# State-space stage of a decoder block: a rotated real scan on VectorE in place of eight levels of shifted matmuls

## What is computed

```python
# 32 groups of 16 channels, 64 complex states for each group, 2048 positions
a_bar = jnp.exp(lam * dt)                          # (32, 64) complex
b_bar = ((a_bar - 1.0) / lam)[..., None] * b
bu = jnp.einsum('bsgc,gpc->bsgp', uf.astype(jnp.complex64), b_bar)
_, states = lax.associative_scan(combine, (a_seq, bu), axis=1)   # s[t] = a_bar * s[t-1] + bu[t]
y = jnp.einsum('bsgp,gcp->bsgc', states, c).real + d_skip * uf
```

## Time and profile before

| what | us |
|---|---|
| median of 3 runs | 3365.31 (3364.07 to 3366.06) |
| the profiled execution | 3363.57 |
| its span in the trace | 3361.8 |
| busy in the span: PE, PEld | 3075.7, 2599.8 |
| busy in the span: DVE, ACT, POOL | 1742.0, 1119.1, 589.3 |

### The profile page before, as it was taken

One profiled execution on the slowest core, in us unless ns is written; L12 is line 12 of the kernel. 1 busy time (PEld: TensorE's weight loads), 2 busy tenths in 40 slices (PEclk: granted clock), 3 DMA queues, 4 the chain that ended last, 5 costly groups with the idle time before them and its releaser, 6 DMA issues. The chain is left out here.

```text
span 3361.8 us, 43581 instructions
## 1 busy us (share of the span) xinstructions
PE 3075.7 (91%) x16178; PEld 2599.8 (77%) x16178; DVE 1742.0 (52%) x2451; ACT 1119.1 (33%) x1919; POOL 589.3 (18%) x387
## 2 busy tenths in 40 slices
PE   6999918969999987995999699999999899999998
PEld 5888816759889976774788578888888788888887
DVE  5333357557778764545566444444444544444444
ACT  4333214537677663312343221111111211111111
POOL 1212246825555541210000000000000000000000
PEclk9999958979999998997999899999999999999999
DMA  4233261072322205414122431111111411111111
GB/s 162 82 89 86 68 84 27 26 179 70 79 54 48 57 15 124 119 63 179 53 94 82 144 112 45 50 50 50 50 50 50 151 50 50 50 50 50 50 37 63
DMA packets 230223, 251.42 MB, mean 75 GB/s; under 512 B 107456, under 2 KB 181184, under 8 KB 230080
## 3 DMA queue, kind: packets, MB, share of 16 engines
q1 hardware_dynamic: 230096, 249.74, 25.3%
HBM read 189.79 MB, written 58.73 MB: 74 GB/s over the span
## 5 line engine op out<-in xcount | busy, mean ns | idle before, releaser
L2474 DVE TENSOR_TENSOR f_y<-f_ps_down,f_y 128x1024 f32<-128x1024 f32 x256 | 313.3, 1224 | 324.4 <-PE f_ps_down L2584 324.4
L2417 ACT ACTIVATE f_act_f<-f_ps_up 128x512 f32<-128x512 f32 x128 | 76.5, 598 | 1030.1 <-PE f_ps_up L2568 1030.1
L2566 PE MATMUL f_ps_up<-f_ht_hi,f_up_hi 128*128 128x512 f32 x1024 | 400.8, 391 | 6.4 <-DVE f_act_f L2491 6.4
L2582 PE MATMUL f_ps_down<-f_down_hi,f_a_hi 128*128 128x512 f32 x1024 | 400.6, 391 | 6.1 <-issue 6.1
L2567 PE MATMUL f_ps_up<-f_ht_lo,f_up_hi 128*128 128x512 f32 x1024 | 400.1, 391 | 0.0
L2568 PE MATMUL f_ps_up<-f_ht_hi,f_up_lo 128*128 128x512 f32 x1024 | 400.0, 391 | 0.0
L2583 PE MATMUL f_ps_down<-f_down_lo,f_a_hi 128*128 128x512 f32 x1024 | 399.9, 390 | 0.0
L2584 PE MATMUL f_ps_down<-f_down_hi,f_a_lo 128*128 128x512 f32 x1024 | 399.7, 390 | 0.0
L690 POOL TENSOR_TENSOR a_w<-a_on,a_left 128x640 f32<-128x640 f32 (+5 forms) x192 | 282.1, 1469 | 254.8 <-DVE a_left L740 113.3
L2491 DVE SCALAR_TENSOR_TENSOR f_act_f<-f_ps_up,f_act_f 128x512 f32<-128x512 f32 x128 | 88.5, 691 | 393.4 <-ACT f_act_f L2417 393.4
L828 PE MATMUL a_ps_y<-a_wt,a_v 128*96 128x128 f32 x2176 | 271.3, 274 | 3.7 <-DVE a_yt L763 3.7
(11 more groups left out here) (319 smaller groups left out, 5738.4 us busy)
## 6 DMA issues: line engine op xcount, KB each, us to landing
f_up_raw<-in_w_up SPq DMA_DIRECT2D x32, 1024.0 KB, 5.3
f_down_raw<-in_w_down SPq DMA_DIRECT2D x32, 1024.0 KB
p_xt<-in_x SPq DMA_DIRECT2D x16, 512.0 KB, 4.8
q<-p_qt SPq DMA_DIRECT2D x16, 512.0 KB, 3.2
k<-p_qt SPq DMA_DIRECT2D x16, 512.0 KB, 3.2
a_q<-q SPq DMA_DIRECT2D x16, 512.0 KB, 5.5
a_k_hi<-k SPq DMA_DIRECT2D x32, 256.0 KB, 8.2
a_k_lo<-k SPq DMA_DIRECT2D x32, 256.0 KB, 9.1
```

The costliest lines, as they stand in the source:

```text
L2474: dve.tensor_tensor(y[:, t, :], down_ps[t % 2][:, :], y[:, t, :], ALU.add).then_inc(added.sem, 1)
L2566: pe.matmul(o, up_hi[:, k, cols], ht_hi[:, k, rows], start=(k == 0), stop=False)
L2582: pe.matmul(o, a_hi[par][:, s, rows], down_hi[:, s, cols], start=(s == 0), stop=False)
```

## The change

In place of the level matrices, the scan is made of real numbers. A chunk's factor is written as `rho` times a rotation. Turning the state of chunk n back by n rotations leaves a recurrence with the real factor `rho`, the same at each step, which `tensor_tensor_scan` on DVE does along the free axis; the result is turned forward again. For this the kernel needs a table of the cosine and the sine of n rotations, for each state and each of 256 chunks.

- Setup: `dbl` is gone. `t_in` and `mat_out` are each made by three or four DVE operations of 4096 elements, `mat_out` all on DVE. DVE makes the first 64 entries of the table for all groups (`low`, by doubling) and the rotations by 64 and 128. ACT copies `mat_in`, a second matrix `mat_in_j` (states with real and imaginary part exchanged) and `kern`. PE makes the exchanged `mat_out_j` in 8 further matmuls through the single bank `o_ps`, ACT copying each out.
- For each pair: ACT copies 64 entries into `table` and multiplies by the rotation (`parts`, four operations for each of two levels), POOL adds the products up to 128 and then to 256 entries (`grow`, two operations for each level). PE makes v and its exchanged form (`make_v`, 4 matmuls in place of 2). DVE multiplies both by the table and adds (`tilt`, `add`), and scans (2 scans of 256). POOL multiplies the result by cosine and by sine (`rotate`, 2 operations of 510 elements). PE makes y with 6 matmuls in place of 4. The 32 matmuls of the levels are gone.
- `u` is kept in three buffers of 8 groups, in place of all 32 groups.

The core of the diff:

```diff
-                pool.tensor_tensor(turned_part[:, :, :], swap[:, None, :].to_broadcast([P, LEVELS, P]),
-                                   dbl[:, :, 1, g:g + 1].to_broadcast([P, LEVELS, P]), ALU.mult
...
-                pool.tensor_tensor(a_mat[g // 2 % 4][:, g % 2, :, :], plain_part[g % 2][:, :, :], turned_part[:, :, :],
-                                   ALU.add).then_inc(a_ready, 1)
...
+            def grow(p):
+                t = table[p % TS]
+                pool.wait_ge(low_copied, p + 1)
...
+                for level, m in enumerate((LO, 2 * LO)):
+                    pool.wait_ge(part_ready, 8 * p + 4 * level + 4)
+                    by_s, by_c = part[:, :, 0, :, 0:m], part[:, :, 1, :, 0:m]
+                    pool.tensor_tensor(t[:, 0, :, m:2 * m], by_c[:, 0, :, :], by_s[:, 1, :, :], ALU.subtract).then_inc(grown, 1)
+                    pool.tensor_tensor(t[:, 1, :, m:2 * m], by_c[:, 1, :, :], by_s[:, 0, :, :], ALU.add).then_inc(grown, 1)
+            def rotate(p):
+                pool.wait_ge(scanned, 2 * p + 2)
...
+                pool.tensor_tensor(s_cos[p % RS][:, :, 1:CHUNKS], t[:, 0, :, 0:CHUNKS - 1], now, ALU.mult
+                                   ).then_inc(rotated, 1)
+                pool.tensor_tensor(s_sin[p % RS][:, :, 1:CHUNKS], t[:, 1, :, 0:CHUNKS - 1], now, ALU.mult
+                                   ).then_inc(rotated, 1)
+            grow(0)
+            grow(1)
+            for p in range(PAIRS):
+                rotate(p)
+                if p + 2 < PAIRS:
+                    grow(p + 2)
...
+            def parts(p):
...
+                act.activation(t[:, :, :, 0:LO], low[:, :, 2 * p:2 * p + 2, :], ACT.Copy).then_inc(low_copied, 1)
+                for level, (m, turn) in enumerate(((LO, turn64), (2 * LO, turn128))):
+                    if 2 * p + level:
+                        act.wait_ge(grown, 4 * p + 2 * level)
+                    for i in range(2):
+                        g = 2 * p + i
+                        src = t[:, :, i, 0:m] if level else low[:, :, g, :]
+                        for by, x in ((0, 1), (1, 0)):
+                            act.activation(part[:, :, by, i, 0:m], src, ACT.Copy, scale=turn[:, x, g:g + 1]
+                                           ).then_inc(part_ready, 1)
...
+            for p in range(PAIRS):
+                if p + 2 < PAIRS:
+                    parts(p + 2)
+                copy_y(p)
...
+            def tilt(p):
+                dve.wait_ge(v_made, p + 1)
+                dve.wait_ge(grown, 4 * p + 4)
...
+            for p in range(PAIRS + 1):
+                if p < PAIRS:
+                    tilt(p)
+                if p >= 1:
+                    scan(p - 1)
+                if p < PAIRS:
+                    add(p)
...
+            for n in range(G // 4):
+                if n >= 1:
+                    pe.wait_ge(crossed_copied, n)
+                mm = pe.matmul(o_ps[:, :].rearrange("p (g l c) -> p g l c", g=4, c=C), swap[:, :], mat_out[:, 4 * n:4 * n + 4, 1:SUB + 1, :],
+                               start=True, stop=True)
+                mm.then_inc(crossed_made, 1)
...
+            for p in range(PAIRS):
+                if p == 0:
+                    make_v(2)
+                    pe.wait_ge(within_in, SUB * DMA)
+                elif p + 2 < PAIRS:
+                    make_v(p + 2)
+                make_y(p)
```

More of the change, by code:

```diff
@@ L884, in ssm_scan @@
-        kern = sb("kern", [C, G, P])
+        mat_out_j = sb("mat_out_j", [P, G, SUB * C])
+        t_in = mat_out_j[:, :, :].rearrange("p g (l c) -> p g l c", c=C)
         mat_within = sb("mat_within", [P, G, P])
[L886 to L897, removed]
+        u = sb("u", [P, US, 8, CHUNKS])
+        table = [sb(f"table{i}", [P, 2, 2, CHUNKS]) for i in range(TS)]
@@ L974, in _ @@
[L974 to L986, removed]
@@ L1006, in _ @@
             act.activation(num[:, 7, :], num[:, 5, :], ACT.Sin, scale=0.5).then_inc(sines, 1)
[L1007 to L1017, removed]
@@ L1048, in stt, with both @@
                 link(dve.scalar_tensor_tensor(out, a, x, b, op0, op1))
-            ROUND = 12582912.0
+            def both(*instructions):
+                for ins in instructions[:-1]:
+                    ins.then_inc(dve_link, 1)
+                    link.n += 1
+                link(instructions[-1])
             def exp_of(out, x, k, r):
@@ new lines, in _ @@
+            dve.wait_ge(in_rows, 1)
+            both(dve.tensor_copy(turn8[:, 0, :], num[:, 9, :]), dve.tensor_copy(turn8[:, 1, :], num[:, 6, :]))
+            for _ in range(3):
+                squared(turn8, turn8)
+            normalise(one(turn8), 1, None)
+            link(dve.tensor_copy(low[:, :, :, 0], turn8[:, :, :]))
+            m = 1
+            while m < LO:
+                first, last = low[:, :, :, 0:m], low[:, :, :, m - 1:m]
+                straight, crossed = [wide[:, i * 2 * G * m:(i + 1) * 2 * G * m].rearrange("p (a g n) -> p a g n", a=2, g=G)
+                                     for i in range(2)]
+                both(dve.tensor_tensor(straight, first, last[:, 0:1, :, :].to_broadcast([P, 2, G, m]), ALU.mult),
+                     dve.tensor_tensor(crossed, first, last[:, 1:2, :, :].to_broadcast([P, 2, G, m]), ALU.mult))
+                both(dve.tensor_tensor(low[:, 0, :, m:2 * m], straight[:, 0, :, :], crossed[:, 1, :, :], ALU.subtract),
+                     dve.tensor_tensor(low[:, 1, :, m:2 * m], straight[:, 1, :, :], crossed[:, 0, :, :], ALU.add))
+                m *= 2
+                if m == 16:
+                    normalise(low[:, :, :, 0:m], m, None)
@@ new lines, in _ @@
+            link(dve.tensor_copy(turn64[:, :, :], low[:, :, :, LO - 1]))
+            normalise(one(turn64), 1, None)
+            squared(turn128, turn64)
+            normalise(one(turn128), 1, None)
+            dve.engine_nop().then_inc(low_ready, 1)
+            dve.wait_ge(in_turned, G // 4)
+            c_of = [cc[:, x, :].rearrange("p (g c) -> p g c", c=C) for x in range(2)]
+            above = pw[:, 1:SUB + 1, :, :]
+            both(dve.tensor_copy(mat_out[:, :, 0, :], c_of[0]),
+                 dve.tensor_tensor(mat_out[:, :, 1:, :], by_row(c_of[0]), by_power(above, 0), ALU.mult),
+                 dve.tensor_tensor(wide4, by_row(c_of[1]), by_power(above, 1), ALU.mult))
@@ new lines, in add, with scan @@
+            def add(p):
+                dve.wait_ge(tilted_j, p + 1)
+                dve.wait_ge(tilted_v, p + 1)
+                dve.tensor_tensor(two(v_ps[p % VS]), two(v_ps[p % VS]), tilted[p % 2][:, :, :], ALU.add).then_inc(added, 1)
+            def scan(p):
+                dve.wait_ge(added, p + 1)
+                if p >= SS:
+                    dve.wait_ge(rotated, 2 * (p - SS + 1))
+                for i in range(2):
+                    g = 2 * p + i
+                    dve.tensor_tensor_scan(sigma[p % SS][:, i, :], rho[:, g:g + 1].to_broadcast([P, CHUNKS]),
+                                           v_ps[p % VS][:, i * CHUNKS:(i + 1) * CHUNKS], 0.0, ALU.mult, ALU.add
+                                           ).then_inc(scanned, 1)
```

324 lines of the change are left out of this document (175 added, 149 removed).

## The result

The changed kernel takes 3374.7 us (median of 7 runs, 3372.8 to 3381.3), the kernel before took 3365.4 beside it (7 runs, 3363.9 to 3371.2). The ratio is 1.0025, with a 95% interval of 1.0015 to 1.0035: slower by 9 us, a little more than the 0.2% that I took as the least that can be told. The profiled execution took 3373.3 us, its span is 3371.5.

What follows compares the result with a forecast made beforehand. PE bounds the loop before, a closed chain across engines afterwards. Loop start 565.2, plus 8.7 to scan 1, 118.0 for 13 periods and 13.5 at the end: 705.4 us, 14.9 later, so 3380.2 us; range 3364 to 3394.

Steps and rivals of the forecast that it cites:

- Setup: Steps ahead of the exchange: `in_rows` at 489.5 us, table's end 516.6, `mat_out` 531.4, `kern` copied by 541.4.
- rival of dear wide operations: Setup: the six stepped 4096-element operations of `t_in` and `mat_out` cost 0.5 ns an element more, +12 us: 3392; chance 0.13.
- Exchange: Before the loop: eight matmuls and copies through one bank cannot overlap; at PE's lower clock they take 19.3 us.
- X: Time when the loop proper starts, behind the exchange: 565.2 us, or 559.2 at 2.4 GHz.
- The chain: Pair loop: rotation, `grow` with ACT's products, tilt and scans run in series, 9.08 us a pair; 13 periods take 118.0 us.
- Tail: Behind scan 14: rotation 14, two `make_y` of 12 instructions each at the lower clock, and the copy, 13.5 us.
- lower bound of 8.0 us: The end of the stage behind scan 14, with PE at 2.4 GHz: 8.0 us in place of 13.5.
- the open chain: Rival in the loop: the chain does not close, POOL's 4.5 us a pair sets the pace, saving 60 us: 3320; chance 0.10.
- PE as the bound: Rival in the loop: PE at the lower clock takes 9.8 us a pair, +9 us more, 3389; chance 0.08.

Runs made afterwards that it cites:

- two-bank run: The changed kernel with the eight exchange matmuls of mat_out going through two PSUM banks in turn, in place of one: 3365.9 us, ratio to before 0.9997.
- scan-first run: The changed kernel with DVE's queue having the scan of a pair ahead of the tilt of the next one: 3342.5 us, ratio to before 0.9928.

## Why the prediction was right

Forecast 3380, measured 3375, and slower as said. The last copy of y was due to end at 705.4 us and ends at 702.9, so 12.4 us later than before where 14.9 were due. In the profiled executions the forecast is 5.2 us too high: 2.5 of it are in the stage, 2.4 in the later stages, which I had taken as equal. Part of how close the number comes is luck, since errors in it offset each other. Point by point:

- **Setup:** `in_rows` due at 489.5, PE's first transpose starts at 490.7; table's end due at 516.6, found at 517.5; `mat_out` due at 531.4, found at 531.5; `kern` copied at 541.4, found at 540.9. Here two errors offset: `t_in` ends 1.1 us late (`bb` starts at 473.3, not 472.1), `mat_out` and `kern` together take 1.4 less than due. The rival of dear wide operations is refuted by 4.42 us where 4.45 was due.
- **Exchange:** due 2.68 us apart at the lower clock, found 2.76. X due at 565.2, found 564.9. The step from there to the first scan's end was 8.2 us, 8.7 due. The two-bank run shows the term by itself.
- **The chain:** 9.08 us a pair due, 9.16 found, link by link in the period shown above. Two errors offset each other. The rotation, priced by L690, was 0.26 us too cheap; L273's shortest, 1.27 us in the same group, was the right row, which I kept as a bound. The 1.3 us that I set beside it and gave to the Trainium skill do not follow from its figure alone: 2.6 cycles an element at the 1.2 GHz with which the same section works are an estimated 1.1 us (GPSIMD Engine Reference, 3.1 Elementwise — side-by-side cycle accounting). The trace agrees with that figure as a slope: L273 and L1483 are 1124 ns apart for 512 elements, an estimated 2.6 cycles each, and leave 0.15 us for each operation. Slope and fixed part together are an estimated 1.27 us for 510 elements, near the 1.26 found. L690 is another line, 638 ns at 256 and 1091 at 512, an estimated 2.1 cycles an element. The other links with their crossings were together 0.18 us too dear. Thirteen periods took 119.4 us, 118.0 were due; one of the thirteen is 9.51 us long, since its tilt starts 0.44 us behind POOL's L1005 and not 0.09; what it waited for is open.
- **Tail:** the term that was mis-sized, 13.5 us due, 10.4 found. I had put all 24 matmuls at the lower clock. The trace has a granted clock of 0.50 from 695 to 698 us and 1.00 from 699 to 702: PE, busy without pause, gets the clock back in the middle of the burst. My lower bound of 8.0 us was added up wrongly, its own terms make 8.4; this bound and my value bracket what was found.
- **Rivals:** the open chain did not happen in the change, and the scan-first run shows what it is worth, 32 us rather than the 60 that I gave it. My 60 took POOL's busy time as the pace; POOL also stands waiting for ACT's products inside its own queue, 1.8 us a pair, and for the next pair's. PE as the bound is refuted: in the loop its clock is 0.83 and it is busy for 86 of 135 us. The low clock does come back in part, as the rival had it: two y matmuls of 256 columns behind a pause of PE of 4.58 us take 1.22 us (630.69), those behind 2.89 us take 0.70 (621.53). But the bursts end in time for the next link.

Not settled: how the 2.4 us by which the later stages differ come about; by the scatter they may be nothing.

## What to carry to other kernels

When engines hand work round in a ring, write down the wait behind each place in each queue before counting loads: here each engine was half idle, and the order of two calls on one of them cost 32 us. When two engines both have all their operands in SBUF, an operation moved from one to the other is worth most if it falls into a pause of the first: 0.90 of 1.13 us with the sine product in POOL's wait, 0.71 of 1.22 with it beside POOL's product. Behind a single PSUM bank, matmul and copy can cost more than their overlap: here the clock stayed at 0.50 as long as PE paused for each copy, and went to 1.00 once two banks took the pauses away.

## What I had not expected of the hardware

- A product of 510 elements on POOL takes 1.26 us with both inputs at the same offset in their buffers and 1.18 with one of them an element further. That this comes from the offset and not from something else in how the buffers lie was not tried apart; the trace has 1.09 for 512 elements in L690.
- Taking turns costs most where the operation is short and the other engine's is long: 128 elements on POOL took 4.63 us beside a DVE operation of 4.68, ten times their 0.45. Making DVE's operations wider made the kernel before slower, 3374 us in place of 3366.
- DVE operations that write PSUM cost what others do: L1267 0.69 us, L1272 0.67 us at 512 elements; a scan of 256 from PSUM costs 0.67.
